# Attention stages of a two-block transformer kernel: token-major queries and keys turned by TensorE, two heads side by side, heads run between the next projections

## The reference

```python
def fox_attention(h, w_in, b_f, q_gain, k_gain, w_out):      # layer 0
    proj = h @ w_in                                          # 16 heads of 64: q, k, v, and one gate per head
    q = rms_norm_2(qkv[:, :, 0], q_gain)                     # over the 64 values of a head
    k = rms_norm_2(qkv[:, :, 1], k_gain)
    cum = jnp.cumsum(jax.nn.log_sigmoid(f_logit), axis=1)
    ...
    logits = q @ k.T * 64 ** -0.5 + cum[q] - cum[k]          # causal
    p = softmax(logits); o = p @ v
    return o @ w_out

def dilated_attention(h, cos, sin, w_in, q_gain, k_gain, w_out):   # layer 1
    # three groups (window, dilation) = (128, 1), (512, 4), (2048, 16), each with its own q, k, v of 16 heads
    q = apply_rope(rms_norm_2(proj[:, :, g, 0], q_gain[g]), cos, sin)   # rope on 16 of a head's 64 values
    ...
    # query t attends t, t-d, t-2d, ..., t-window; the three outputs are merged by their softmax denominators
    return o.reshape(B, S, H * hd) @ w_out
```

## Time and profile before

| | |
|---|---|
| median of 3 runs (range) | 3151.91 us (3149.42 to 3152.05) |
| the profiled execution, and its span | 3153.38 us, 3151.7 us |
| mean granted clock of TensorE | 0.964 of full speed |
| PE, PEld, DVE, ACT busy | 2978.7, 2799.4, 2074.5, 1425.4 us |
| attention of layer 0, first projection to first residual of the last output tile | 1951.65 to 2137.67 us |
| attention of layer 1, the same | 2545.22 to 2949.86 us |

### The profile page before, as it was taken

The page is one execution under the profiler, slowest core; times in us unless marked ns, Lnnn a source line. Parts: engine busy times, 40 slices in busy tenths (PEclk is TensorE's granted clock), DMA queues, the critical chain, the costliest instruction groups (busy, mean ns, idle before and its releaser), DMA issues.

```text
span 3151.7 us, 60793 instructions
## 1 busy us (share of the span) xinstructions
PE 2978.7 (95%) x26520; PEld 2799.4 (89%) x26520; DVE 2074.5 (66%) x2939; ACT 1425.4 (45%) x2144; POOL 13.5 (0%) x23
## 2 busy tenths in 40 slices
PE   7999899899999998998999899999999999988999
PEld 7999777799999987787999899879999988877899
DVE  5666556666666665566666666756666679886554
ACT  4445444344444454343444444534444454545443
POOL 0000000000000000000000000000000000000000
PEclk9999999999999998999999999989999999989999
DMA  6664211246666632112466465305656643420344
GB/s 225 237 242 163 106 42 42 103 166 241 233 219 237 223 147 94 42 46 104 174 247 238 171 236 210 147 28 192 236 201 253 242 155 136 155 100 1 130 178 147
DMA packets 72649, 511.26 MB, mean 162 GB/s; under 512 B 8192, under 2 KB 8960, under 8 KB 11584
## 3 DMA queue, kind: packets, MB, share of 16 engines
q1 hardware_dynamic: 72384, 507.37, 43.3%
HBM read 506.29 MB, written 1.05 MB: 161 GB/s over the span
## 4 chain that ended last, share of the span: by engine, by line
PE 86%; DVE 8%; ACT 4%; issue 1%; DMA 0%; SPq 0%; DVEq 0%; ACTq 0%
PE linear_banks L1693 23%; PE linear_banks L1694 22%; PE linear_banks L1695 22%; PE linear_banks L1989 1%; PE solve_banks L2023 1%; PE solve_banks L1756 1%; DVE qk_rstd L1563 1%; PE solve_banks L2032 1%; PE linear_banks L1739 1%; PE linear_banks L1741 1%; PE linear_banks L1740 1%; DVE split_halves L1116 1%; PE solve_banks L2145 1%; DVE rstd L1131 1%; DVE logits L1611 1%
## 5 line engine op out<-in xcount | busy, mean ns | idle before, releaser
L1116 DVE TENSOR_TENSOR split_halves<-raw_units,split_halves 128x1024 fp32r<-128x1024 f32 x806 | 978.5, 1223 | 543.7 <-ACT split_halves L759 540.8
L1693 PE MATMUL linear_banks<-h_split,split_halves 128*128 128x256 f32 x4256 | 1238.9, 291 | 60.1 <-DVE h_split L1148 26.8
L1694 PE MATMUL linear_banks<-h_split,split_halves 128*128 128x256 f32 x4256 | 1217.3, 286 | 0.0
L1695 PE MATMUL linear_banks<-h_split,split_halves 128*128 128x256 f32 x4256 | 1216.7, 286 | 0.0
L759 ACT ACTIVATE split_halves<-raw_units 128x1024 fp32r<-128x1024 f32 x806 | 848.8, 1057 | 732.0 <-PE linear_banks L1695 626.7
L1693 PEld LDWEIGHTS linear_banks<-h_split,split_halves 128*128 128x128 f32 x4256 | 829.5, 195 | 84.6 <-issue 59.5
L1694 PEld LDWEIGHTS linear_banks<-h_split,split_halves 128*128 128x128 f32 x4256 | 830.4, 195 | 3.2 <-issue 3.1
L1695 PEld LDWEIGHTS linear_banks<-h_split,split_halves 128*128 128x128 f32 x4256 | 829.9, 195 | 0.0
L1693 PE MATMUL linear_banks<-hidden_split,split_halves 128*128 128x256 f32 x1408 | 397.4, 282 | 0.0
L1694 PE MATMUL linear_banks<-hidden_split,split_halves 128*128 128x256 f32 x1408 | 394.7, 280 | 0.0
L1695 PE MATMUL linear_banks<-hidden_split,split_halves 128*128 128x256 f32 x1408 | 394.7, 280 | 0.0
(11 more groups left out here) (288 smaller groups left out, 3500.9 us busy)
## 6 DMA issues: line engine op xcount, KB each, us to landing
raw_units<-in_stream SPq DMA_DIRECT2D x403, 1024.0 KB, 4.8
raw_units<-in_mod_w SPq DMA_DIRECT2D x72, 1024.0 KB, 6.7
x<-in_x SPq DMA_DIRECT2D x4, 256.0 KB, 4.7
w2a<-in_w2a SPq DMA_DIRECT2D x2, 512.0 KB, 6.0
w_rows<-in_w SPq DMA_DIRECT2D x2, 512.0 KB, 7.3
bs_rows<-in_bs SPq DMA_DIRECT2D x2, 512.0 KB, 8.5
spatial_t<-in_ws_t SPq DMA_DIRECT2D x2, 512.0 KB, 9.5
out<-x SPq DMA_DIRECT2D x4, 256.0 KB, 5.0
```

The source lines that it names most:

```text
L1116: V.tensor_tensor(split[:, n % SPLIT_SLOTS, 1, :], raw[:, item % RAW_SLOTS, (n % 2) * HALF * P:(n % 2 + 1) * HALF * P], split[:, n % SPLIT ...
L1693: M(o, w_hi, a_hi, start=start, stop=False, skip_group_check=skip)
L1694: M(o, w_hi, a_lo, start=False, stop=False, skip_group_check=skip)
L1695: return M(o, w_lo, a_hi, start=False, stop=stop, skip_group_check=skip)
```

## The change

**Projections.** All attention units, q and k too, are computed token-major, one half per call (`tokens_half`). A unit is four heads of q, or of k, or of v. The order of units is now set by `TILES`: in layer 0 the gates first, then q, k, v of heads 0 to 3, of heads 4 to 7, and so on; in layer 1 q and k of the three groups and then v of the three, again by four heads. The number of units is the same (13 and 36).

**Norm and rope of q and k.** With tokens on the partitions a head's square sum is a DVE reduction along the row (128 x 1024, 16 results), the root and the reciprocal are of 128 x 16, and rope touches 16 of 64 columns, with tables that hold cosine, sine and gain. Then PE transposes q and k of four heads (8 transposes of 128 x 128, "turn"), and ACT copies them to `qk` with the gain.

**Heads.** A task is now one block of 128 queries of two heads (16 tasks in a layer). The two heads of a pair use the two row halves of the array for the logits, in two banks, and the two column halves for the values, in one bank. The decay of layer 0 comes from one row of sums per head by a one-hot stationary matrix of 64 rows. In layer 1 the tokens are ordered by their remainder modulo 4 (`h_out`, `h_in`; `residual` puts them back), so the second and the third group need only the 128 keys of the query's own block: 512 key columns for a task. In layer 0 the first query block takes 128 keys, the second 256.

**Order.** `attention_steps` lists the steps: step x begins with half x of the weights, followed by what else is put there. Tasks of heads 4s to 4s+3 run between the projections of the next four heads. When the halves end, four "fill" steps make the first part of the output projection (4 of 8 features' tiles in layer 0, 6 of 8 in layer 1) between the last tasks. PE now waits for all eight tiles of `h_split` before the first projection.

```diff
+TOKENS = np.arange(T).reshape(T // 4, 4).T.reshape(T)
+TILES = ([("f", 0, 0)] + [(kind, s, 0) for s in range(4) for kind in "qkv"],
+         [(kind, s, g) for s in range(4)
+          for kind, g in [(a, b) for b in range(GROUPS) for a in "qk"] + [("v", b) for b in range(GROUPS)]])
...
+            for b in range(GROUPS):
+                n = GROUPS * s + b
+                after(x + 4 * b + 4, "reduce", n)
+                after(x + 4 * b + 5, "root", n)
+                after(x + 4 * b + 5, "norm", n)
+                after(x + 4 * b + 8, "turn", n)
...
+                    y = x + 18 + 4 * i
+                    task(4 * s + i, y, y + 1, y + 3, y + 4)
...
+    order = ("values", "o", "turn", "probs", "logits", "copy", "gate", "gate_log", "gate_sum", "decay", "reduce", "exp",
+             "scale", "root", "norm")
...
+    def h_out(n, part, c):
+        o = h[:, part, c, :]
+        return o.rearrange("p (r i) -> p i r", r=4) if n == 11 else o
...
+                    elif step == "turn":
...
+                            ins = nc.scalar.activation(qk[:, s % 2, g, i, :, :], sv[:, 2 + i, :], ACT.Copy, scale=gain)
...
+                        for hh in range(2):
+                            lg = logits[:, n % 2, hh, 0:w]
+                            ins = nc.scalar.activation(lg, lg, ACT.Exp, scale=HD ** -0.5, bias=st[:, 2 + hh:3 + hh],
+                                                       accum_out=st[:, 4 + hh:5 + hh])
...
-                    link(V.reciprocal(ssr[:, b, :, :], ssr[:, b, :, :]))
...
+                        V.tensor_reduce(qk_ms[:, m % 2, :], qk_squares[:].rearrange("p i (a t) -> p (i a) t", t=HD),
+                                        AX.X, ALU.add).then_inc(reduced, 1)
...
+                V.tensor_tensor(lg, sv[:, 0:2, 0:w], wide(amask[:, at_:at_ + w], 2), ALU.add).then_inc(logits_read, 1)
+                dve.wait_ge(logits_read, m + 1)
+                link(V.tensor_reduce(st[:, 0:2], lg, AX.X, ALU.max, negate=True))
...
-                    M(bank, head_w, pieces[:, p % 2, :, :], start=True, stop=True).then_inc(lin_filled, 1)
...
-                        M(bank, rope_m[:], qkg[:, (DT * g + c) % 2, :, :], start=True, stop=True).then_inc(lin_filled, 1)
...
+                ready = h_wait(8 + 3 * l)
+                for k in range(DT):
+                    ready(k)
+                for step, n in ATTENTION[l]:
+                    if step == "half":
+                        kind = TILES[l][n // 2][0]
+                        tokens_half(base + n, ("tile", l, n // 2), n % 2, HEADS if kind == "f" else 2 * P)
+                    elif step == "fill":
+                        part_of_out(l, n, 0, FILL_K[l])
...
+                    for g in range(GROUPS):
+                        for hh in range(2):
+                            at_ = (0, T, T + P)[g]
+                            keys = k_of(g, hh) if g == 0 else k_of(g, hh)[:, j * CH:(j + 1) * CH]
+                            ins = M(sv[:, hh, at_:at_ + (T if g == 0 else P)], q_of(g, hh), keys, start=True, stop=True)
...
+                for b, (g, i) in enumerate(blocks):
+                    for hh in range(2):
+                        head = 2 * (c % 2) + hh
+                        o = o_bank[64 * hh:64 * hh + 64, j * CH:(j + 1) * CH]
+                        ins = M(o, vtok[:, s % 2, g, i, head * HD:(head + 1) * HD], pt[:, n % 2, hh, b * P:(b + 1) * P],
+                                start=(b == 0), stop=(b == len(blocks) - 1), skip_group_check=True)
```

More of the change, by code:

```diff
@@ L56 @@
         _at += _n
[L57 removed]
+for _name, _n in (("final_norm", 8), ("norm_g", 48), ("fox_g", 2), ("dil_g", 6)):
     COL[_name] = _at
@@ new lines, in attention_steps, with after, task @@
+def attention_steps(l):
+    at = {}
+    def after(half, step, n):
+        at.setdefault(half, []).append((step, n))
+    def task(n, logits, exp, probs, values):
+        after(logits, "logits", n)
+        after(exp, "exp", n)
+        after(exp, "scale", n)
+        after(probs, "probs", n)
+        after(values, "values", n)
+        if n % 2:
+            after(values, "o", n // 2)
+    for u in range(len(TILES[l])):
+        after(2 * u + 1, "copy", u)
+    if l == 0:
+        after(2, "gate", 0)
+        after(2, "gate_log", 0)
+        after(3, "gate_sum", 0)
+        after(6, "decay", 0)
+        for s in range(4):
+            x = 2 + 6 * s
+            after(x + 4, "reduce", s)
+            after(x + 5, "root", s)
+            after(x + 5, "norm", s)
+            after(x + (7 if s < 3 else 6), "turn", s)
+            for i, y in enumerate((8, 9, 11, 12) if s < 3 else (7, 8, 10, 11)):
+                task(4 * s + i, x + y, x + y + 1, x + y + 2, x + y + 3)
+    else:
+        for s in range(4):
+            x = 18 * s
+            for b in range(GROUPS):
[4 more added lines that the diff above has]
+                after(x + 4 * b + 8, "turn", n)
+            for i in range(4):
+                if s < 3:
+                    y = x + 18 + 4 * i
+                    task(4 * s + i, y, y + 1, y + 3, y + 4)
+                else:
+                    y = x + (17, 18, 20, 21)[i]
+                    task(4 * s + i, y, y + 1, y + 2, y + 3)
+    order = ("values", "o", "turn", "probs", "logits", "copy", "gate", "gate_log", "gate_sum", "decay", "reduce", "exp",
+             "scale", "root", "norm")
+    halves = 2 * len(TILES[l])
+    steps = []
+    for half in range(max(at) + 1):
+        if half < halves:
+            steps.append(("half", half))
+        elif half < halves + 4:
+            steps.append(("fill", half - halves))
+        steps += sorted(at.get(half, []), key=lambda step: order.index(step[0]))
+    return steps
@@ L103, in group_norm_at @@
+ATTENTION = [attention_steps(l) for l in range(2)]
+TURN_USE = {}
+for _l in range(2):
+    for _step, _n in ATTENTION[_l]:
+        if _step in ("turn", "probs"):
+            TURN_USE[_step, _l, _n] = len(TURN_USE)
 def group_norm_at(c, i):
@@ L267, in make_plan @@
         p.stream(("mix", 2 + l), (13, 36)[l])
-        for g in range((1, 3)[l]):
-            for c in range(DT):
-                p.use(("qk", l, g, c), "act")
-                if c:
-                    p.use(("ss", l, g, c - 1), "act")
-                    if l:
-                        p.use(("rot", l, g, c - 1), "dve")
-                if c % 2:
-                    p.use(("v", l, g, c // 2), "act")
-            p.use(("ss", l, g, DT - 1), "act")
-            if l:
-                p.use(("rot", l, g, DT - 1), "dve")
-        if l == 0:
-            p.use(("f", 0), "dve")
-        for c in range(DT):
-            p.use(("o", l, c), "dve")
+        for step, n in ATTENTION[l]:
+            if step == "half" and n % 2 == 0:
+                p.use(("tile", l, n // 2), "dve" if TILES[l][n // 2][0] == "f" else "act", at_once=False)
+            elif step == "half":
+                p.fill(("tile", l, n // 2))
+            elif step == "copy" and TILES[l][n][0] != "f":
+                p.empty(("tile", l, n))
+            elif step == "gate":
+                p.empty(("tile", 0, 0))
+            elif step == "decay":
+                p.use(("decay", 0), "dve")
         p.stream(("out", 2 + l), 4)
@@ L1024, in attention @@
-                for g in range(ng):
-                    for c in range(DT):
-                        keep_ahead(half + 1)
-                        half += 2
-                        bank = wait_filled(act, ("qk", l, g, c))
-                        square(("ss", l, g, c), pairs(bank))
-                        n = DT * (g + l) + c
-                        if n >= 2:
-                            act.wait_ge(qk_ready, n - 1)
+                    nc.scalar.activation(cos16[:, :, 0:8], cos[:], ACT.Sin).then_inc(rope_ready, 1)
```

601 lines of the change are left out of this document (321 added, 280 removed).

## The result

The changed kernel takes 3054.59 us, median of 4 runs (3053.73 to 3055.44). The kernel before, run beside it, took 3151.98 us (3149.42 to 3154.89). The ratio is 0.969, 95% interval 0.967 to 0.971: 97 us less. The forecast was 3040, its range 3008 to 3088. In the profiled executions (3153.38 and 3053.73) the gain is 99.7 us, where the sum had 113.9.

What follows compares the result with a forecast made beforehand. PE, busy 95% of the span, was taken as the bound. Its work and waits summed to 159.8 us in layer 0 (26.2 less) and 316.9 in layer 1 (87.7 less), from 3153.4 to 3039.5, stated as 3040; range 3008 to 3088.

Steps and rivals of the forecast that it cites:

- The two wide products: Both layers' square sums and layer 1's rope products, 512 columns each on PE; their removal was to save 48.2 us.
- The rival of the pairs: In the heads, two heads side by side do not overlap on PE; 38 us more, 3078; chance 0.1.
- the chain: Rival: in both layers the chain DVE to ACT sets the pace; 60 us more, 3100; chance 0.12.
- the slow one: Rival: each task's chain stands fully in PE's way, projections and heads not overlapping; 64 us more, 3216; chance 0.04.
- Start: Beginning of each attention: PE waits for the last tile of h and begins 5.5 us later in each layer.
- after the longer pause I take 1.7: Behind the norm of each layer: low clock costs 1.7 us, up from 1.4 us lost before.
- Tail: After the last half, four tasks remain: 7 us idle in layer 0, 8 in layer 1, and 3 each for clock.
- the 25 and 35 us named as a sign of being wrong: Sign: the tail from the last half to the last values exceeds 25 us in layer 0 or 35 in layer 1.
- Middle: Where heads run between projections, PE waits 7 us in layer 0 and 3 in layer 1; bounds 0 and 30 over both.
- waits are covered: Rival: the added waits are covered, idle and clock terms of 31 us shrink to 5; 3014; chance 0.15.
- shape change of 0.2 us: PE's cost per change of array shape, about 50 in each layer, 10 us a layer.
- The strides: Layer 1's 64-column steps in h and the residual's PSUM reads: taken as nothing, bound 8 us; rival 3048, chance 0.04.

Runs made afterwards that it cites:

- e2: Changed kernel with the logits of both heads of a pair on the same row half of the array: 3079.0 us, 25 more.
- e4: Changed kernel with the root of q's and k's square sums replaced by an exponential, so ACT loads no table between: 3049.5 us, 4 less.
- e3: Changed kernel with all of layer 0's head tasks behind its projections and no output projection between them: 3091.6 us, 38 more.
- e6: Changed kernel with tasks 14 and 15 of both layers one half earlier in the order: 3051.2 us, 2.5 less.
- e1: Changed kernel with layer 0's first unit of q computed ahead of the gates: 3055.2 us, ratio to the kernel before 0.969.
- e9: Changed kernel with the gates' product 256 columns wide instead of 16, 240 of them zeros: 3055.4 us, layer 0 3.2 us less.
- e10: Changed kernel with 256-column gates, the last logits one half earlier and a tile-by-tile start of the first products: 3035.37 us, ratio to before 0.9627.

## Why the prediction was right, and where its sizes were off

**The mechanism.** Right in the middle, where PE's own work sets the pace; at both ends waits and the clock count for more than forecast. The two wide products, the slow heads and half of each pair are gone, and DVE's reciprocal takes 0.25 us where it took 3.35. The rival of the pairs is out for the logits by e2, the chain by e4 and by the middle's 154.9 us busy of 156 in layer 1, the slow one by the result. e3 shows what the order alone is worth in layer 0.

**The size.** Forecast stages were 159.8 and 316.9 us; measured are 168.2 and 326.1, so 8.4 and 9.2 more. Three terms make this up.

- *Start.* The 5.5 us of later start were 6.0 in layer 0 and 7.6 in layer 1, where the strided parts of h make the norm 1.6 us longer. For the low clock I took 1.7. The first three halves took 15.5 us in layer 0 where the sum has 8.2, so 7.3 lost; in layer 1 11.2 for 8.6, so 2.6. Together 6.1 and 3.0 us more than forecast. The failed step is "after the longer pause I take 1.7": it was read from wide products behind a short pause and given to the narrow ones of the gates.
- *Tail.* I took 7 and 8 us idle and 3 each for the clock. From the stretches above, idle is 9.5 + 1.7 = 11.2 us in layer 0 and 10.3 + 1.3 = 11.6 in layer 1; the clock cost 20.5 x 0.10 + 22.7 x 0.15 = 5.5 and 27.7 x 0.24 + 16.8 x 0.06 = 7.6. That is 6.7 and 8.2 more, within the bounds given for the clock, but both stretches went past the 25 and 35 us named as a sign of being wrong: 33 from the last half to the last values in layer 0, 36 in layer 1. The wait that I had not seen is 4.1 us in layer 1, for the division of a task whose logits come late in the order; e6 halves it.
- *Middle.* The waits of 7 and 3 us were 3.1 and 1.7: 3.9 and 1.3 less. The rival "waits are covered" was half right here (4.8 us left of 10) and wrong at both ends.

The sums are 8.9 and 9.9 against 8.4 and 9.2, so all of PE's work together (pairs, turns, shape changes) was priced within 1 us a stage. With the 3.4 us outside, 3039.5 + 17.6 - 3.4 = 3053.7, the profiled time. The total came nearer than the parts: the ends took 24 us more than forecast, and the middle gave 5 back.

**Slips in the working.** Taking the shape change of 0.2 us out of the row-half pair gives (1.11 - 0.2) / 1.72 = 0.53, not the 0.6 used. With 1.08 us for a task's logits of layer 1 the kernel after has (1.08 - 0.2) / 1.71 = 0.51, so the sum had 2 us too much there. In the slow rival, 7.2 us with turns and units is 224.5 in layer 1, not 232; that rival's price is 57 us, 3209. Neither moves the range.

**The strides.** Half right. A low part takes 0.66 us for 0.49 with the step, a pair of residuals reads PSUM with it in 1.24 us where it takes 0.88 in layer 0:

```profile
2117.34 0.88 DVE L1323 SCALAR_TENSOR_TENSOR x<-linear_banks,residual_gate,x 128x256 f32<-128x256 f32 x2 [0.51 <-PE linear_banks L1795]
...
2850.16 1.24 DVE L1323 SCALAR_TENSOR_TENSOR x<-linear_banks,residual_gate,x 128x256 f32<-128x256 f32 x2 [0.44 <-PE linear_banks L1795]
```

On the path that is 1.6 us in the norm and 0.4 at the last residual, of the 8 in the bound; the norm of layer 1 stayed under the 2 us named as the sign. The Trainium skill, "SBUF — State Buffer", section "Door 1: The DMA port swizzle", says that an access which crosses into a new 16-byte line of SBUF pays a penalty. The trace agrees in direction for the parts of h: a low part takes a third longer, 0.66 us for 0.49.

**Not settled.** Why the granted clock at 400 to 450 us, and in the tail of layer 0, differs between executions; how the 78.5 us of layer 1 divide between the new order and the lost products (e3 has layer 0 only); whether the column halves alone make the values' 1.03 us; what the clock does with a product between 16 and 256 columns wide, since no other width was run.

## What to carry to other kernels

When dependent work is threaded between dense products, price its middle by PE's work alone and put the doubt at both ends: the first product behind the norm and the last tasks took 24 us more than forecast, the middle 5 less. Let the first product wait tile by tile, and put the last long chain as early in the order as its buffers allow. A narrow product where the clock matters is worth a trial at a greater width: here 256 columns, 240 of them of zero weights, took 11.0 us with the half behind them where 16 columns took 15.5.

## What was not expected of the hardware

- The granted clock stood at 0.50 for the 10.2 us of the 16-column products, with PE busy 4.00 of 4.00 us, and for another 5.3 us of the 256-column product behind them. In e1 it fell from 0.98 to 0.50 during them. With 256 columns behind the same pause it was at 1.00 within 8 us (e9).
- A matmul of 16 columns started every 0.21 us there, as one of 256 columns does at the low clock (0.21 in e10 too). Making the product 16 times wider cost nothing then.
- 24.3 us of table loads on ACT in a stretch of 248 us cost 2.5 us (e4). In the middle of layer 1 they stand beside projections that keep PE busy.
